# A one-core diffusion block: final scaling on VectorE alone, the last unit's sums at a later place, another order of first loads

## The reference, cut to what matters

```python
xs = xs + g2x[:, None, :] * _swiglu(_modulate(_rmsnorm(xs, norm2_g[l]), sh2x, sc2x), w_ff1[l], w_ff3[l], w_ff2[l])
...
def _swiglu(h, w1, w3, w2):
    a = jnp.einsum('bnd,df->bnf', h, w1)
    g = jnp.einsum('bnd,df->bnf', h, w3)
    return jnp.einsum('bnf,fd->bnd', jax.nn.silu(a) * g, w2)
...
def _rmsnorm(x, g):
    xf = x.astype(jnp.float32)
    y = xf * lax.rsqrt(jnp.mean(xf * xf, axis=-1, keepdims=True) + EPS)
    return (y * g.astype(jnp.float32)).astype(x.dtype)
...
return _rmsnorm(xs, final_g)
```

## Time and profile before

| what | value |
|---|---|
| median of 3 runs (lowest to highest) | 1747.03 us (1745.67 to 1747.12) |
| profiled execution, whole | 1742.91 us |
| its span, first to last instruction | 1741.1 us |
| TensorE matmul busy | 1695.4 us, 97% |
| VectorE busy | 1284.6 us, 74% |
| ScalarE busy | 692.3 us, 40% |
| GpSimd busy | 461.4 us, 27% |
| up projection's last product ends, `plain_down` starts | 1502.3, 1502.8 us |
| first of the ten passes starts, last ends | 1524.7, 1722.5 us |

### The profile page before, as it was taken

The page is one execution under the profiler, slowest core; times in us unless marked ns, Lnnn a source line. Parts: engine busy times, 40 slices in busy tenths (PEclk is TensorE's granted clock), DMA queues, the critical chain, the costliest instruction groups (busy, mean ns, idle before and its releaser), DMA issues.

```text
span 1741.1 us, 23413 instructions
## 1 busy us (share of the span) xinstructions
PE 1695.4 (97%) x8360; PEld 1426.2 (82%) x8360; DVE 1284.6 (74%) x1807; ACT 692.3 (40%) x1135; POOL 461.4 (27%) x410
## 2 busy tenths in 40 slices
PE   6999999999999999999999999999999999999995
PEld 3798988989898888888888888888888888877884
DVE  6687636566456667766788756888788989699996
ACT  7534231423233223445554413533433333423435
POOL 1102020200212000111122200066365546465543
PEclk9999999999999999999999999999999999999998
DMA  9111111202069023787685633256655556976652
GB/s 341 49 50 37 61 49 49 72 24 73 12 215 322 33 97 117 268 293 251 238 301 175 210 129 124 75 176 217 226 204 185 205 208 230 332 252 196 194 158 97
DMA packets 145425, 284.93 MB, mean 164 GB/s; under 512 B 9363, under 2 KB 96035, under 8 KB 141507
## 3 DMA queue, kind: packets, MB, share of 16 engines
q1 hardware_dynamic: 115314, 177.30, 30.6%
q0 software_dynamic: 30032, 106.59, 17.2%
HBM read 205.68 MB, written 78.17 MB: 163 GB/s over the span
## 4 chain that ended last, share of the span: by engine, by line
PE 77%; DVE 11%; DMA 5%; issue 4%; ACT 2%; SPq 1%; POOL 0%; DVEq 0%; ACTq 0%; POOLq 0%
PE PD L2497 14%; PE PM L2945 10%; PE PD L2945 10%; PE PD L2820 4%; PE PD L2982 4%; PE PM L2820 4%; PE PM L2982 4%; PE PD L2851 4%; PE PD L2628 4%; PE PD L2513 4%; DMA g_ring<-g_dram 2%; PE PM L2701 2%; PE PD L2641 1%; PE PM L2881 1%; PE PD L2881 1%
## 5 line engine op out<-in xcount | busy, mean ns | idle before, releaser
L1082 POOL TENSOR_TENSOR wm_lo<-wm_lo,wm_hi 128x1024 fp32r<-128x1024 f32 x35 | 92.9, 2676 | 84.8 <-ACT wm_hi L1590 84.7
L2497 PE MATMUL PD<-R_hi,whi 128*128 128x512 f32 x352 | 110.2, 394 | 0.0
L2497 PE MATMUL PD<-R_lo,whi 128*128 128x512 f32 x352 | 108.5, 390 | 0.0
L2497 PE MATMUL PD<-R_hi,wlo 128*128 128x512 f32 x352 | 108.5, 389 | 0.0
L2263 DVE TENSOR_TENSOR ws_lo<-S,ws_hi 128x512 fp32r<-128x512 f32 x76 | 83.6, 1110 | 20.8 <-ACT ws_hi L1525 20.7
L933 POOL TENSOR_TENSOR kw<-ktok,hc 128x1280 f32<-128x1280 f32 x8 | 18.4, 2322 | 286.6 <-DVE ktok L1947 286.6
L2403 DVE TENSOR_TENSOR fm_lo<-fm_lo,fm_hi 128x512 fp32r<-128x512 f32 x70 | 88.7, 1268 | 3.6 <-ACT fm_hi L1597 3.6
L1525 ACT ACTIVATE ws_hi<-S 128x512 fp32r<-128x512 f32 x76 | 47.7, 628 | 94.1 <-DVE S L2277 63.8
L2497 PEld LDWEIGHTS PD<-R_lo,whi 128*128 128x128 f32 x352 | 66.1, 188 | 13.9
L2497 PEld LDWEIGHTS PD<-R_hi,wlo 128*128 128x128 f32 x352 | 66.1, 188 | 13.9
L2497 PEld LDWEIGHTS PD<-R_hi,whi 128*128 128x128 f32 x352 | 65.2, 188 | 13.0 <-issue 0.2
(11 more groups left out here) (534 smaller groups left out, 5371.7 us busy)
## 6 DMA issues: line engine op xcount, KB each, us to landing
rawF<-in_w_ff SPq DMA_DIRECT2D x44, 512.0 KB, 6.0
wm_lo<-w_dram SPq DMA_DIRECT2D x35, 512.0 KB, 4.1
ada<-in_w_ada POOLq DMA_DIRECT2D x32, 512.0 KB, 5.5
raw<-in_w_in SPq DMA_DIRECT2D x30, 512.0 KB, 4.7
g_dram<-snapG POOLq DMA_DIRECT2D x48, 256.0 KB, 4.8
f_dram<-Fo SPq DMA_DIRECT2D x11, 1024.0 KB, 4.8
w_dram<-job_a POOLq DMA_DIRECT2D x20, 512.0 KB, 3.7
fm_lo<-fs_dram SPq DMA_DIRECT2D x40, 256.0 KB, 4.1
```

Of the source, the lines that this page charges most:

```text
L1082: nc.gpsimd.tensor_tensor(lo[:, :, :], lo[:, :, :].bitcast(F32), hi[:, :, :].bitcast(F32), ALU.subtract).then_inc(wm_ready, 1)
L2497: i = mm(dst[:, e * HALF:e * HALF + width], wk[:, k, :], part, start=(k == 0 and step == 0), stop=(k == KT - 1 and step == 2))
```

## The change

Three edits.

1. The final scaling: every tile is now scaled by VectorE's `write_out`, one instruction with factor and `final_g`, right behind its `norm_factor`. ScalarE's `times_factor` and GpSimd's multiplication go, as does `ylast`. For tiles 0, 4, 1 and 5 this stands between VectorE's sums of the last pass (behind its 3rd, 5th, 7th and 9th), for tile 2 behind the 12th, for tiles 6, 3 and 7 behind the last. The stores wait on VectorE alone.
2. `left_job` of unit 4 moves on GpSimd from before `wm_low(1)` to behind `wm_low(2)`.
3. SP's first loads: four tiles of `xs2` in place of eight, then weights 2 and 3, the first four `fm_lo`, then the other four tiles of `xs2`, weights and `fm_lo` 4 and 5, the store of `Fo`, and the rest. The semaphores of `fm_lo` are others now, so that the first four loads no longer wait for tiles of `xs2`.

```diff
--- before.py
+++ after.py
@@ -94,7 +94,7 @@
 LAST_ORDER = ((0, 0), (1, 0), (0, 1), (0, 2), (1, 1), (0, 3), (1, 2), (0, 4), (1, 3), (0, 5), (1, 4), (0, 6),
               (1, 5), (1, 6))
 ORDER = (0, 2, 3, 1, 5, 4, 6)
-POOL_TILES = (0, 4, 1, 5, 2, 6)
+NORM_TILES = (0, 4, 1, 5, 2, 6, 3, 7)
 LEFT_AT = {0: (0, 0), 1: (1, 0), 6: (1, 1)}
 LAST = (2 * NS - 1) * PRODUCTS
 KH = KT // 2
@@ -346,8 +346,6 @@
                 f_raw0 = sb("f_raw0", [P, 2, NLAT], stack=s7)
                 fg = sb("fg", [P, D], stack=s7)
                 junkF = sb("junkF", [P, D], stack=s7)
-            with ExitStack() as s7:
-                ylast = sb("ylast", [P, D], stack=s7)
             rawF.append(sb("rawF1", [P, KT, CW], stack=sF))
             snap = [sb(f"snap{i}", [P, HALF], stack=sF) for i in range(4)]
             with ExitStack() as s7:
@@ -585,14 +583,14 @@
         job_in, JOBS_IN = fg_in, 32 * len(jobs) + 16
         job_out = sem("job_out")
         wm_in, of_place = ada_in[0:PRODUCTS], 48
-        fm_in, of_xs = x_in[0:PRODUCTS], 32
+        fm_in = [ada_in[KT - 1], vec_in, w2_in, f_in, x_in[0], x_in[1], x_in[2]]
+        of_fm = [16, 16 * 9, 16, 16, 32, 32, 32]
         wm_hi_d, of_scaled = v_scaled, LT
         wm_ready = sem("wm_ready")
         fm_hi_d, of_out = out_mm, 2 * LT
         fm_ready = sem("fm_ready")
         made, of_made = [pl_silu, xn2_done], (4, LT)
         taken = [sem(f"taken{k}") for k in range(2)]
-        factor, normed, o_pool = T_mm, wspT_done, mod_ready
         down_hi_d = sem("down_hi_d")
         down_ready = sem("down_ready")
         down_done = sem("down_done")
@@ -810,7 +808,7 @@
                     src = f_dram[:, 4 * u + 2 + 2 * kh:4 * u + 4 + 2 * kh, at:at + CW]
                 else:
                     src = fs_dram[:, u, n - 2, :, g * CW:(g + 1) * CW]
-                sp.wait_ge(fm_in[p], of_xs + 16 * (2 * u + g))
+                sp.wait_ge(fm_in[p], of_fm[p] + 16 * (2 * u + g))
                 sp.dma_start(fm[p][1][:, g, :, :].bitcast(F32), src).then_inc(fm_in[p], 16)
 
             def up_done(n):
@@ -827,22 +825,30 @@
             for p in range(2):
                 load_w(0, p)
             up_done(4)
-            for t in range(LT):
-                sp.dma_start(xs2[:, t, :], xs_dram[:, t, :]).then_inc(x_in[t], 16)
+            def load_xs(first, end):
+                for t in range(first, end):
+                    sp.dma_start(xs2[:, t, :], xs_dram[:, t, :]).then_inc(x_in[t], 16)
+
+            load_xs(0, 4)
             up_done(5)
-            for p in range(2, 6):
+            for p in range(2, 4):
                 load_w(0, p)
             up_done(PRODUCTS)
-            for p in range(6):
+            for p in range(4):
+                load_f(0, 0, p)
+            load_xs(4, LT)
+            for p in range(4, 6):
+                load_w(0, p)
                 load_f(0, 0, p)
             sp.wait_ge(f_made, NS + 1)
+            sp.dma_start(f_dram[:, NBLK - 2:NBLK, :], Fo[:, :, :]).then_inc(f_out, 16)
             load_w(0, 6)
-            sp.dma_start(f_dram[:, NBLK - 2:NBLK, :], Fo[:, :, :]).then_inc(f_out, 16)
-            for p in range(6):
+            for p in range(2):
                 load_f(0, 1, p)
             sp.wait_ge(f_out, 16 * NFB)
-            for g in range(2):
-                load_f(0, g, 6)
+            load_f(0, 0, 6)
+            for p in range(2, PRODUCTS):
+                load_f(0, 1, p)
             for G in range(2 * DU - 1):
                 u, g = G // 2, G % 2
                 for p in range(PRODUCTS):
@@ -854,14 +860,12 @@
                         if u + 1 == DU - 1:
                             sp.wait_ge(job_out, stores["f", DU - 1])
                         load_f(u + 1, g, p)
-            for i, t in enumerate(POOL_TILES):
-                sp.wait_ge(o_pool, i + 2)
+            for i, t in enumerate(NORM_TILES[0:7]):
+                sp.wait_ge(o_ready, i + 2)
                 sp.dma_start(out_t[:, t, :], xs2[:, t, :]).then_inc(out_done, 16)
-            sp.wait_ge(o_ready, 2)
-            sp.dma_start(out_t[:, 3, :], xs2[:, 3, :]).then_inc(out_done, 16)
             for i, e in enumerate((1, 0)):
                 at = slice(e * HALF, (e + 1) * HALF)
-                sp.wait_ge(o_ready, 3 + i)
+                sp.wait_ge(o_ready, LT + 1 + i)
                 sp.dma_start(out_t[:, LT - 1, at], xs2[:, LT - 1, at]).then_inc(out_done, 16)
             sp.wait_ge(out_done, 16 * (LT + 1))
 
@@ -1096,14 +1100,10 @@
             pool.wait_ge(down_done, LT + 1)
             pool.dma_start(fg[:, :], final_g.rearrange("(o n) -> o n", o=1).to_broadcast([P, D]))\
                 .then_inc(fg_in, 16)
-            left_job(len(jobs) - 1, DU - 1, job_down)
             for u in range(1, DU):
                 wm_low(u)
-            pool.wait_ge(fg_in, JOBS_IN)
-            for i, t in enumerate(POOL_TILES):
-                pool.wait_ge(normed, i + 2)
-                nc.gpsimd.tensor_tensor(xs2[:, t, :], xs2[:, t, :], fg[:, :], ALU.mult).then_inc(o_pool, 1)
-
+                if u == 2:
+                    left_job(len(jobs) - 1, DU - 1, job_down)
 
         @block.scalar
         def _(act):
@@ -1593,7 +1593,7 @@
 
                 u, g = G // 2, G % 2
                 hi, lo = fm[p]
-                act.wait_ge(fm_in[p], of_xs + 16 * (G + 1))
+                act.wait_ge(fm_in[p], of_fm[p] + 16 * (G + 1))
                 nc.scalar.activation(hi[:, g, :, :], lo[:, g, :, :].bitcast(F32), ACT.Copy).then_inc(fm_hi_d, 1)
 
             def up(q, par, following):
@@ -1639,13 +1639,6 @@
                 nc.scalar.activation(rs[:, 3, t:t + 1], rs[:, 0, t:t + 1], ACT.Identity, scale=-0.5 / D, bias=half)\
                     .then_inc(root_d, 1)
 
-            def times_factor(i, col):
-
-                t = POOL_TILES[i]
-                act.wait_ge(factor, i + 2)
-                nc.scalar.activation(xs2[:, t, :], xs2[:, t, :], ACT.Copy, scale=rs[:, 2, col:col + 1])\
-                    .then_inc(normed, 1)
-
             def half_square(t, e, i):
 
                 par, late = t % 2, t >= KH
@@ -1662,22 +1655,17 @@
                 else:
                     root(col, last_at[i], last_half_at[i])
 
-            for i, t in enumerate(POOL_TILES[0:4]):
+            for t in NORM_TILES[0:4]:
                 par = t % 2
                 act.wait_ge(taken[par], (2 * DU - 1) * PRODUCTS_ADDS)
                 own.link(nc.scalar.activation(junkF[:, :], xs2[:, t, :], ACT.Square, accum_out=rs[:, 0, t:t + 1]))
                 root(t, eps_at, eps_half_at)
-                if i > 0:
-                    times_factor(i - 1, POOL_TILES[i - 1])
-            times_factor(3, POOL_TILES[3])
             half_square(2, 0, 0)
             half_square(6, 1, 1)
             half_square(3, 0, 2)
             half_square(2, 1, 0)
             half_square(7, 1, 3)
-            times_factor(4, LT)
             half_square(6, 0, 1)
-            times_factor(5, LT + 1)
             half_square(3, 1, 2)
             half_square(7, 0, 3)
 
@@ -2439,11 +2427,7 @@
                 dve.wait_ge(root_d, 2 * roots + 1)
                 own.link(v.reciprocal(y, root))
                 own.link(v.scalar_tensor_tensor(out=root, in0=y, scalar=half, in1=y, op0=ALU.mult, op1=ALU.mult))
-                return v.scalar_tensor_tensor(out=y, in0=root, scalar=1.5, in1=y, op0=ALU.add, op1=ALU.mult)
-
-            def pool_factor(i, col):
-
-                norm_factor(col, i + 1).then_inc(factor, 1)
+                own.link(v.scalar_tensor_tensor(out=y, in0=root, scalar=1.5, in1=y, op0=ALU.add, op1=ALU.mult))
 
             def write_out(t, at, col):
                 v.scalar_tensor_tensor(out=xs2[:, t, at], in0=xs2[:, t, at], scalar=rs[:, 2, col:col + 1],
@@ -2454,19 +2438,19 @@
             for n, (par, p) in enumerate(LAST_ORDER):
                 take(END, par, p)
                 if n in (2, 4, 6, 8):
-                    i = n // 2 - 1
-                    pool_factor(i, POOL_TILES[i])
+                    t = NORM_TILES[n // 2 - 1]
+                    norm_factor(t, n // 2)
+                    write_out(t, whole, t)
                 if n == 11:
-                    pool_factor(4, LT)
-                if n == 12:
-                    pool_factor(5, LT + 1)
-                    own.link(v.tensor_tensor(ylast[:, parts[1]], xs2[:, LT - 1, parts[1]], fg[:, parts[1]], ALU.mult))
-            own.link(norm_factor(LT + 2, 7))
+                    norm_factor(LT, 5)
+                    write_out(2, whole, LT)
+            norm_factor(LT + 1, 6)
+            write_out(6, whole, LT + 1)
+            norm_factor(LT + 2, 7)
             write_out(3, whole, LT + 2)
-            own.link(norm_factor(LT + 3, 8))
-            v.tensor_scalar(xs2[:, LT - 1, parts[1]], ylast[:, parts[1]], rs[:, 2, LT + 3:LT + 4], None, ALU.mult)\
-                .then_inc(o_ready, 1)
-            write_out(LT - 1, parts[0], LT + 3)
+            norm_factor(LT + 3, 8)
+            for e in (1, 0):
```

(1 more changed line is left out.)

## The result

| | median us | runs | ratio to before, 95% interval |
|---|---|---|---|
| before, beside it | 1745.67 | 5 | |
| changed | 1733.51 (1732.39 to 1737.23) | 5 | 0.9936, 0.992 to 0.9953 |

The kernel is faster, by 11 us by the ratio. The ratio forecast, 1732.7 / 1747.0 = 0.9918, lies just outside the interval, and that of rival (a), 0.9948, inside it. The trace says why: one part of the forecast had the wrong sign. The traced execution took 1735.71, its span 1734.0 against 1741.1.

A forecast was written before the change was run, and what follows sets the result against it. TensorE was taken to bound the kernel, so only its standing time and the stretch after its last matmul pay. 7.4 + 2.0 + 5.2 = 14.6, less 0.3 for refills, gave 1747.0 - 14.3 = 1732.7; range 1730.5 to 1739.5.

The forecast's parts named there:

- rival (a): At the moved sums' new place: the stall moves with them, `wm_lo` again following stores; cost 5.2, 1737.9; chance 0.25.
- The final scaling, 7.4: After TensorE's last matmul: one VectorE scaling instruction per tile replaces ScalarE's and GpSimd's multiplications; gain 7.4 us.
- the low price: Final scaling: VectorE's scaling instruction beside ScalarE's squares taken at 1.21 us per tile, with 2.4 as the bound above.
- rival (c): Kernel's end: the scaling is dearer or the last stores bunch up, halving the tail's gain; 1736.4; chance 0.08.
- The first loads, 2.0: Before pass 0: earlier `fm_lo` loads remove TensorE's two waits there, 1.6 us plus 0.4 of refilling.
- rival (b): First loads bring nothing, since VectorE's `fm_lo` still meet six `wm_lo` in a row; 1734.7; chance 0.08.
- The moved sums, +5.2: Pass 2: unit 1's `wm_lo` then run without a TensorE wait; gain 2.9, 1.7 and 0.6 of refilling, 5.2 us.
- Cost 0 by that: New place, pass 6: VectorE's sum falls 2.8 us behind its product, a bank being wanted after 3.4; so no cost.
- the 4.1 us: Base of the forecast: the median of the kernel before lies 4.1 us above its profiled execution.
- Rival (d): Around unit 3: VectorE misses its turn again and again, each miss costing TensorE 5.2; slower, 1753; chance 0.05.
- (e): One miss at unit 3 and the scaling at the dear price: within 3.5 of before, 1745; chance 0.04.
- the upper bound: Final scaling: at 2.4 us per scaling instruction, eight tiles cost 9.5 us more, turning the 7.4 gain into a loss of 2.

The follow-up runs named there:

- the extra wait: GpSimd takes up each `wm_lo` subtraction only after its own last one; added to the kernel before 0.9963, the changed one 0.9913, the changed one without the move 0.9909.
- batch 3: Third group of runs sharing runs of the kernel before (median 1744.27): first loads alone 0.9963, move undone 0.9924, three `wm_lo` held ready 0.9924, the same behind four stores 0.9997.
- the extra stores: Changed kernel, move undone, GpSimd held before unit 3's `wm_lo` until three are ready, then issuing the last unit's four stores a second time: 1743.2, 0.9997.
- batch 1: First group of runs sharing runs of the kernel before (median 1745.39); the changed kernel again there: 1735.54, ratio 0.9944.
- the stores late: Changed kernel with the moved sums' four stores issued behind unit 3's `wm_lo` instead of ahead of them: 1730.27, ratio 0.9919.
- the sums put back: Changed kernel with the last unit's sums back before unit 1's `wm_lo`, scaling and first loads still changed: 1727.59, 0.9901; second set 1730.24, 0.9924.

## Why the prediction was right, and where it was not

**The final scaling, 7.4: right.** 7.0 measured alone (4.5 to 9.4 by the interval). Step by step: tiles 0, 4, 1 and 5 were to be done at 1710.05, 1713.1, 1716.1 and 1719.8; shifted by the 0.65 us that TensorE ends later (1723.15 against 1722.5), the trace agrees to within 0.1 each (the first 1709.47 + 1.29 = 1710.76). The scaling takes 1.28 or 1.29 on every tile, beside ScalarE's squares, so the low price held and rival (c) falls. VectorE never waits for a root. The Trainium skill's advice in "Perfetto Trace Analysis", section "Optimizing Scalar/DVE Operations", to hand work of a saturated VectorE to ScalarE or GpSimd, does not bear against the change: the windows show VectorE busy 8.43 of 18.5 us in the old tail, and the tail 7.7 us shorter with the work moved onto it.

**The first loads, 2.0: the step right, the worth too small.** Both waits of pass 0 are gone as told, and rival (b) falls. The gain alone is 6.5 to 9.1. The part beyond 2.0 seems to belong to the stall of pass 2, by two comparisons. Where the extra wait has taken that stall away, scaling and first loads together bring 0.9963 less 0.9909, 9.4 us in one batch, which is 7.4 + 2.0; without the wait the same two edits bring 17.3 (13.3 in batch 3). And with the stall present, the new order changes how many `wm_lo` meet the stores. GpSimd's sums begin 18.4 to 19.0 us after the first product in the three traces with the old order, and 14.8 to 17.1 in seven with the new one. In the three of these that begin before 15, two `wm_lo` are ready, not three, and the `fm_lo` is 4.3 instead of 6.3 to 6.7. The row of one:

```profile
1552.46 4.76 POOL L1086 TENSOR_TENSOR wm_lo<-wm_lo,wm_hi 128x1024 fp32r<-128x1024 f32 x2
```

How often that is so, and whether some executions lose more than the traced ones, is not shown; that the whole difference lies there is inferred.

**The moved sums, +5.2: wrong in sign.** Measured, the move costs 3.5 to 7.5 us. Two steps failed. The first is "Cost 0 by that" for the new place. The arithmetic of times was good: the sums end at 1629.3, 8.4 us ahead of pass 6 (1523.4 + 6 x 19.04 = 1637.6), where the forecast had 6 to 10 ahead of 1646.3, and unit 3's `wm_lo` were in time. But it counted the new place's `wm_lo` as in the kernel before, spread out and alternating with VectorE, whereas they now came directly behind stores, four on end (three in the second trace). That is rival (a), which was named and given 0.25. With the extra wait in place the move does cost next to nothing (0.9913 against 0.9909 without the move, from two batches). Its price was low too: 5.2, against 9.3 us that TensorE loses in the passes (199.8 less 190.5), of which 5.4 are waits, 13 matmuls at 0.43 instead of 0.2265 are 2.6, and the rest is refilling. The other failing step was to add three terms as if they were independent: by the medians the first loads already took much of the stall that the move was to take, though no trace shows it gone by them alone.

**"Against" rival (a)**: five other back-to-back runs in which VectorE came in. All five were true and beside the point, since none followed stores of GpSimd. The one run that did was the long one. The Trainium skill, "SBUF — State Buffer", section "Who interferes with whom", was cited with the remark that by it alone (a) is void. It was not void. The section says that the two engines block each other for the whole instruction, and the usual 1.70 agrees; the trace of the kernel with the extra stores has one VectorE instruction held until seven of GpSimd's are done, 15.61 us, which the rule does not give, and the measurement decides.

**Sum and base.** Forecast 14.3, measured 11.2 in the first comparison and 9.8 in batch 1. The 9.8, split by the first two batches: 7.0 for the scaling, 10.3 for the first loads (17.3 for both less 7.0), and 7.5 lost to the move. So the first loads brought 8.3 more than forecast and the move 12.7 less; the two errors cancelled in large part, and that the time came out better than its reasons is luck. What was forecast as the passes' length, 191 us, is what the changed kernel has without the long `fm_lo`: 190.6 with the extra wait, 190.9 with the stores late. And the 4.1 us put between the traced execution and the median was no constant: in the changed kernel the traced one lies 2.2 above the median. Rival (d) was not met: the event comes once per batch of stores, not again and again. Nor was (e), whose miss came but not its dear scaling; its 1745 is also no sum of its terms, since 1732.7 + 5.2 + 3.7, the dear price of (c), is 1741.6, and with the 9.5 of the upper bound it is 1747.4.

## What to carry to other kernels

When a stall is explained by one event, write down the whole sequence around it (here: stores issued by GpSimd, ready GpSimd instructions behind them, a VectorE instruction with both inputs in SBUF) and look for that sequence at the place to which the work moves; counterexamples count only if they share all of it. Let GpSimd wait for its own last instruction behind DMAs that it issued, or issue them later: here neither cost anything, and with the wait the executions lay closer together. And two remedies for one stall don't add up: price the second as if the first were in.

## What the hardware showed that was not expected

- GpSimd's instructions without a gap, directly behind four DMAs that it issued: VectorE's two-input SBUF subtraction is kept out until GpSimd stops. It ends 0.54 to 0.57 us after GpSimd's last one in all eleven cases of ten traces, and so it is as long as what was left of the run when it began: 4.3 us with two, 6.3 to 6.7 with three, 7.8 with four, 15.6 with seven (and 7.92 with three where it began 0.26 us ahead of the first); GpSimd runs at 2.34 to 2.38 each. Without the DMAs, or with a wait for its own last instruction in between, they alternate: 1.70 and 2.74 to 2.76, the longest `fm_lo` 3.2. Why a DMA issued ahead should matter, and whether one is enough, was not tried.
- Much of the scatter between executions of one kernel (8 to 10 us with the first loads or the sums put back) is probably this event; the traces show it in two lengths, not how often each comes. With it gone the executions lie 1.3 to 1.6 us apart in the two changed versions with the wait (4.4 with the stores late, 3.7 in the kernel before with the wait). But the changed kernel, with the event in both its traces, lies within 2.4 in one set, and the start of the passes alone differs by up to 4 us between traces.
- TensorE's 10.64 us of standing were followed by twelve matmuls and more at the lower clock level (1.2 GHz, granted clock 0.50 in the window from 1650 to 1660), 0.43 us apart instead of 0.2265, so that such a wait costs some 3 us more than its length. Timeline and window of that stretch:

```profile
1655.48 0.63 PE L2974 MATMUL PD<-wm_lo,fm_hi 128*128 128x512 f32 x1
1655.91 0.63 PE L2974 MATMUL PD<-wm_hi,fm_lo 128*128 128x512 f32 x1
```

```profile
1650.00:1660.00 10.00, 5.08 (x12) 4.05 (x13) 8.46 (x11) 1.04 (x3) 1.82 (x1) 0.50 0.00 0
```
